# A first block of a transformer: another order for its opening stage, and two RMS norms' inverse roots moved from the operands to the products

## The chip, the cores and the metric

The kernel runs on one core of one Trainium2 chip. The metric is device time in microseconds (us) of one execution. Three runs of the kernel before gave 2043.5, 2043.73 and 2045.62 us, so the median is 2043.73 us. Engines: PE is the matrix engine (PEld its weight loads), DVE the vector engine, ACT the scalar engine, POOL the general engine, SP the engine that issues most transfers.

## The reference, cut to what matters

```
h = rmsnorm(x, norm_mix);  x = x + s5_mixer(h, ...)          # state space model, gelu, y @ w_glu, a * sigmoid(g)
x = x + sqrelu_mlp(rmsnorm(x, norm_ffn), mlp_w1, mlp_w2)     # relu(h @ w1)^2 @ w2
gate = sigmoid(rmsnorm(x, norm_ple) @ ple_gate_w);  x = x + (p @ ple_w) * gate
x = rmsnorm(x, norm_final)
... two more layers (w_ada_2 modulation, four mixer branches, swiglu), final norm
rmsnorm(x, g) = x * rsqrt(mean(x*x) + eps) * g               # mean over the 1024 features of a token
```

x is 256 tokens by 1024 features, everything in float32. The mixer is a linear recurrence with 64 groups of 16 features and 64 complex states, run here over 32 chunks of 8 tokens.

## The kernel before, in words

Each engine runs its own hand-written program, and semaphores tie them together. All big products ("phases" glu, mlp1, mlp2, ple and then those of the two layers) go through `gemm_pe` (L2487). A weight block of 1 MB lands in one of four ring slots of `raw`. ACT rounds each half of it into `wh` (`split_hi`, L799), POOL subtracts for the rest, `wl` (L2478), and PE takes three products per tile: xh\*wh, xl\*wh, xh\*wl (L2490 to L2492). SP loads the ring in the order of `RINGSEQ`: slot g is loaded again when block g-4 is used. Between the weights stand the 48 blocks of `w_ada`, each used once by `ada_block` (L649, 16 matmul records). Blocks 0 to 11 come first in the ring, ahead of the glu weights. After glu and after mlp2 come three blocks (`ada_tail`, run at the end of `gemm_pe`), then two weight blocks of the next phase, then a fourth ada block, whose slot is that of the second of the three.

**Opening.** While x loads, PE runs five unread products (`warm(5, 3)`, L2557, two records each). Then it transposes x (L2564) and x by group (L2570, which ends in `s_U`), the C matrices (L2578, `s_ct5`), the chunk factors (L2583) and the vectors (L2588). DVE builds b (to L2836), the factors F in four groups (`f_group`, 8.8 us each with a scratch in PSUM), U (L2895, after group 0), two products for the skip gain (L2902), the scan over chunks S (L2941 to L2959) and the last quarter of E (`e_group(3)`, L2855 to L2857). POOL builds the other three quarters of E. PE turns F pair by pair (`w1_transposes`, L2600), ACT copies each pair (L2294), PE multiplies it with U (`v_products`, L2611), and ACT copies V (L2285). Ada blocks 0, 1 and 2 come after pairs 8, 16 and 24. Then `k_products` (L2635, two halves), the skip product (L2660), `k_back` (L2648), which gives the lags K that ACT copies (L2306), and ada blocks 3, 4, 5. SP waits for that copy before it goes on with ring block 7, and issues seven transfers that shift the lags into the Toeplitz operand `toep` (`toep_dma`, L621). SP filled `toep` with zeros earlier, after `s_ct5` (L733), and only then began the ring. `y_products(d)` for d = 0 to 7 (L2682 with toep, L2687 with S and E) waits for S and toep; ada blocks 6 to 11 stand between them. For each d DVE turns Y (L2966), and ACT and DVE take turns for the gelu: square (L2310), argument (L2973), tanh (L2314), gate (L2978), xh (L2319), xl (L2982). Glu's first products need xh, xl of d = 0 to 7 one after the other.

**Norms 0 and 1** stand between glu and mlp1, and between mlp2 and ple. `norm_pe` (L929) takes sums of squares (L946, L951), five unread products (L926), spreads the inverse roots over the partitions (`norm_spread_pe`, L966) and runs the fourth ada block (`late`). DVE has the root chain (`rms_head_dve`, L1012) and then per feature tile x \* gain \* root (L1112), ACT rounds that to xh (L1094), DVE subtracts for xl (L1123). Mlp1 starts when the first tile is there.

Of the kernel before, what the change touches and what calls it, by code (L numbers as in the profile page):

```python
# [106 lines left out]
def build(nc, A, out, spill):  # L107
    ctx = ExitStack()
    with ctx:
# [119 lines left out]
        wsq = sqr[:, 2, SEQ:2 * SEQ]  # L229
        arena2 = part_m.mark[0]  # L230
# [131 lines left out]
        s_T = sem("toeplitz_placed")  # L362
# [18 lines left out]
        s_r = sem("relu_ready")  # L381
# [175 lines left out]
        HOME = {0: 40, 1: 40, 7: 40, "layer": 40}  # L557
# [29 lines left out]
        TOEP_AT = 7  # L587
# [28 lines left out]
        def toep_dma(sp):  # L616

            sp.wait_ge(s_Kc, 2)
# [40 lines left out]
        def ada_select(pe, i):  # L659

            pe.wait_ge(s_ac, i + 1)
            for b in range(2):
                ins = nc.tensor.matmul(ada_out[i][:, 32 * b:32 * b + 32], adat[:, b * P:b * P + P],
                                       const[:, C_SEL:C_END], start=True, stop=True)
            ins.then_inc(s_at, 1)

# [13 lines left out]
        def _(sp):  # L680
# [53 lines left out]
            for g in range(len(RINGSEQ)):  # L734
# [3 lines left out]
                if g == TOEP_AT:  # L738
                    toep_dma(sp)
# [362 lines left out]
        def norm_dve(dve, T1, n, gain, ring, dg, shift=None):  # L1102
# [6 lines left out]
            for k in range(KD + 1):  # L1109
# [7 lines left out]
                if k:  # L1117
# [11 lines left out]
                    ins.then_inc(s_xl, 1)  # L1129

# [1086 lines left out]
        def _(act):  # L2217
# [36 lines left out]

            def f_row_zero(r):
# [5 lines left out]
                for ri in range(2):  # L2261
                    nc.scalar.copy(Fg[r][:, :, ri, 0, :], Bb[:, ri, 8 * r:8 * r + 8, :]).then_inc(s_F0, 1)

            act.wait_ge(s_ct5, 1)
# [3 lines left out]
            act.wait_ge(s_fp5, 1)  # L2268
            nc.scalar.copy(fac[:, :], gb[:, 3, 0:NCH]).then_inc(s_fac, 1)

            f_row_zero(0)
            f_row_zero(1)
            act.wait_ge(s_vt, 1)
            nc.scalar.copy(vecs[:, :], gb[:, 1, 0:480]).then_inc(s_vc, 1)
            act.wait_ge(s_vc, 1)
            act.wait_ge(s_vz, 2)
            A1.add(nc.scalar.activation(sc[:, :, 30:31], vecs[:, V_C:V_C + 8].rearrange("p (k o) -> p k o", o=1),
                                        ACT.Tanh, scale=0.5))
            A1.add(nc.scalar.activation(sc[:, :, 31:32], vecs[:, V_CC:V_CC + 8].rearrange("p (k o) -> p k o", o=1),
                                        ACT.Tanh, scale=0.5))  # L2280
            A1.wait()
            act.sem_inc(s_th, 1)
            def v_copy(r):
                act.wait_ge(s_w1u, 8 * (r + 1))
                nc.scalar.copy(V[:, :, :, 8 * r:8 * r + 8].rearrange("p c r q -> p q r c"),  # L2285
                               mb[:, r, :].rearrange("p (q r c) -> p q r c", r=2, c=NCH)).then_inc(s_Vc, 1)

            f_row_zero(2)
            f_row_zero(3)
            for q in range(PAIRS):  # L2290
                act.wait_ge(s_w1t, q + 1)
                if q >= 4:
                    act.wait_ge(s_w1u, q - 3)
                nc.scalar.copy(w1[:, q % 4, :, :], gb[:, 1 + q % 2, 0:256].rearrange("p (r m) -> p r m", r=2))\  # L2294
# [4 lines left out]
            for i, banks in enumerate((gb[:, 1:3, :], mb[:, 2:4, :])):  # L2299
                act.wait_ge(s_KT, i + 1)  # L2300
                nc.scalar.copy(KT[:, 2 * i:2 * i + 2, :, :], banks.rearrange("p b (r n) -> p r b n", r=2))\
                    .then_inc(s_KTc, 1)
            act.wait_ge(s_K, 1)
            lags = toep[:, CH - 1, :, :].rearrange("p (q b) h -> p b q h", b=2)
            for b in range(2):
                nc.scalar.copy(lags[:, b, :, :], mb[:, b, :].rearrange("p (q h) -> p q h", h=GH)).then_inc(s_Kc, 1)  # L2306

            def gelu_square(d):
                act.wait_ge(s_yv, d + 1)
                nc.scalar.activation(gl[:, d % 2, 1, :], gl[:, d % 2, 0, :], ACT.Square).then_inc(s_y2, 1)  # L2310
# [6 lines left out]
            def gelu_hi(d):  # L2317
                act.wait_ge(s_yg, d + 1)
                nc.scalar.mul(xh[:, d, home("glu", SEQ)], gl[:, d % 2, 3, :], 0.5).then_inc(s_xh, 1)  # L2319

            for d in range(KD):
# [4 lines left out]
                if d == 5:  # L2326
                    act.wait_ge(s_E, 4)
                    act.wait_ge(s_S, 1)
                if d > 4:
                    for h in ((0, 1), (0,), (1,))[d - 5]:  # L2330
                        split_hi(act, (p_glu, 0, (0, 1, 1)[d - 5]), h)

            gelu_hi(KD - 1)
            ada_copy(act, 0)
            gemm_act(act, p_glu, pair_tanh(act, p_glu, SEQ), tail=lambda: squares_act(act, 0, sqr), split_first=False)
            act.dma_start(pnat[:, :, :], A["p"][0, 0].rearrange("(a p) d -> p a d", p=P)).then_inc(s_p, 16)
            operand_act(act, 0, sqr)
# [10 lines left out]
            gemm_act(act, p_m2, lambda it, j: None, tail=lambda: squares_act(act, 1, sqr), split_first=False)  # L2348
# [4 lines left out]
            operand_act(act, 1, sqr)  # L2353
# [14 lines left out]
            gemm_act(act, p_pl, pair_tanh(act, p_pl, SEQ), context_copy,  # L2368
# [118 lines left out]
        def gemm_pe(pe, p, T, X, need=None, after=None, lead=()):  # L2487
# [23 lines left out]
            def turn(it):  # L2511
                for j in range(p.body):
# [8 lines left out]
                    for b in range(2):  # L2521
# [10 lines left out]
                        ins.then_inc(mm_done, 1)  # L2532
                    i = it * p.body + j
# [11 lines left out]
        def _(pe):  # L2545
# [14 lines left out]
            warm(5, 3)  # L2560
# [12 lines left out]
            pe.wait_ge(s_x1, 1)  # L2573
            pe.wait_ge(s_cnat, 16 * 8)
# [5 lines left out]
            pe.wait_ge(s_small, 32)  # L2580
            pe.wait_ge(s_chk, 1)
            for a in range(2):
                ins = nc.tensor.matmul(gb[:, 3, GH * a:GH * a + GH], const[:, REP:CHK], chk[:, a, :], start=True, stop=True)  # L2583
            ins.then_inc(s_fp5, 1)
# [174 lines left out]
        def _(dve):  # L2759
# [226 lines left out]
            for d in range(KD + 1):  # L2986
                if d < KD:
                    turn_y(d)
# [110 lines left out]
```

## Time and profile before

| what | value |
|---|---|
| median of 3 runs | 2043.73 us |
| the profiled execution's own time | 2041.48 us |
| its span | 2039.7 us |
| PE busy | 1927.6 us, 95% |
| DVE, ACT, POOL busy | 932.9, 750.5, 1113.1 us |
| granted PE clock, mean | 0.965 of full |
| the opening, to the first glu product | 129.6 us |
| glu's last product, mlp1's first | 186.0 us, 198.3 us |
| mlp2's last product, ple's first | 410.7 us, 423.5 us |

"Busy" is the sum over an engine's instructions. The granted clock is a share of full speed: 0.50 is 1.2 GHz, 1.00 is 2.4 GHz. PE is busy for all but 112 us of the span.

### The profile page before, as it was taken

How to read it: one execution, taken by the hardware profiler on the slowest of the kernel's cores; microseconds unless marked ns; L12 is line 12 of the kernel's file. 1: busy time of each engine (PE TensorE's matmuls, PEld its weight loads, DVE VectorE, ACT ScalarE, POOL GpSimd, SP SyncE). 2: the span in 40 equal slices, each digit the busy share in tenths (PEclk: the TensorE clock that was granted, in tenths of full speed). 3: DMA queues.
4: the chain of work that ended last, by engine and by line, in shares of the span. 5: the costliest groups of instructions: out<-in, count | busy, mean ns of one | idle time of the engine just before them, and what ended most of it. 6: DMA issues, size and time to landing. Idle time of an engine off the chain costs nothing.

```text
span 2039.7 us, 33055 instructions
## 1 busy us (share of the span) xinstructions
PE 1927.6 (95%) x13867; PEld 1697.2 (83%) x13867; DVE 932.9 (46%) x1677; ACT 750.5 (37%) x1209; POOL 1113.1 (55%) x611
## 2 busy tenths in 40 slices
PE   6879999989999999999999999999999998989997
PEld 4558899987988689878777888888898997989997
DVE  7955441164555693662344111113557756363112
ACT  4333443233233722452323222222335526434443
POOL 6536777764344544344352444444368754777885
PEclk7779999999999999899998999999999999999999
DMA  7376788876213032212421323322255331555653
GB/s 162 117 259 218 262 285 270 278 247 218 80 46 107 14 114 73 63 32 93 144 93 62 104 78 109 103 80 85 90 159 156 110 109 32 179 167 165 183 179 101
DMA packets 299706, 276.72 MB, mean 136 GB/s; under 512 B 19771, under 2 KB 296773, under 8 KB 299301
## 3 DMA queue, kind: packets, MB, share of 16 engines
q1 hardware_dynamic: 297044, 271.43, 42.3%
q10 hardware_dynamic: 2192, 2.77, 0.4%
q8 instruction: 110, 1.80, 0.4%
q0 software_dynamic: 320, 0.40, 0.1%
q14 instruction: 40, 0.32, 0.0%
HBM read 266.70 MB, written 4.19 MB: 133 GB/s over the span
## 4 chain that ended last, share of the span: by engine, by line
PE 83%; DVE 8%; ACT 3%; POOL 2%; issue 2%; DMA 2%; SPq 1%; DVEq 0%; ACTq 0%; POOLq 0%
PE gb L2490 18%; PE gb L2492 17%; PE gb L2491 17%; PE gb L1443 4%; PE gb L1445 4%; PE gb L1444 4%; PE gb L1667 3%; PE gb L1669 3%; PE gb L1668 3%; PE mb L649 2%; POOL wl L2478 2%; PE mb L1175 1%; ACT wh L799 1%; PE mb L1242 1%; DMA raw<-in_w_ada 1%
## 5 line engine op out<-in xcount | busy, mean ns | idle before, releaser
L2478 POOL TENSOR_TENSOR wl<-raw,wh 128x1024 fp32r<-128x1024 f32 (+3 forms) x452 | 980.9, 2188 | 836.5 <-ACT wh L799 836.3
L799 ACT CAST wh<-raw 128x1024 fp32r<-128x1024 f32 (+3 forms) x452 | 418.9, 938 | 738.4 <-PE gb L2492 357.1
L2490 PE MATMUL gb<-xh,wh 128*128 128x256 f32 (+1 forms) x1856 | 604.3, 326 | 16.5 <-DVE xl L1125 6.7
L2491 PE MATMUL gb<-xl,wh 128*128 128x256 f32 (+1 forms) x1856 | 599.9, 323 | 0.0
L2492 PE MATMUL gb<-xh,wl 128*128 128x256 f32 (+1 forms) x1856 | 599.6, 323 | 0.0
L2490 PEld LDWEIGHTS gb<-xh,wh 128*128 128x128 f32 x1856 | 352.3, 190 | 55.5 <-issue 14.9
L2492 PEld LDWEIGHTS gb<-xh,wl 128*128 128x128 f32 x1856 | 352.2, 190 | 27.7
L2491 PEld LDWEIGHTS gb<-xl,wh 128*128 128x128 f32 x1856 | 352.4, 190 | 27.2
L1443 PE MATMUL gb<-wh,xh 128*128 128x256 f32 x608 | 174.7, 287 | 1.4 <-POOL wl L2478 1.3
L1444 PE MATMUL gb<-wh,xl 128*128 128x256 f32 x608 | 172.9, 284 | 0.0
L1445 PE MATMUL gb<-wl,xh 128*128 128x256 f32 x608 | 172.8, 284 | 0.0
L1443 PEld LDWEIGHTS gb<-wh,xh 128*128 128x128 f32 x608 | 117.5, 193 | 3.3 <-issue 3.2
L1667 PE MATMUL gb<-fhh,wh 128*128 128x512 f32 (+1 forms) x352 | 118.2, 336 | 0.0
L1444 PEld LDWEIGHTS gb<-wh,xl 128*128 128x128 f32 x608 | 117.5, 193 | 0.3 <-issue 0.2
L1669 PE MATMUL gb<-fhh,wl 128*128 128x512 f32 (+1 forms) x352 | 117.8, 335 | 0.0
L1668 PE MATMUL gb<-fhl,wh 128*128 128x512 f32 (+1 forms) x352 | 117.7, 334 | 0.0
L1445 PEld LDWEIGHTS gb<-wl,xh 128*128 128x128 f32 x608 | 117.4, 193 | 0.0
L2166 DVE SCALAR_TENSOR_TENSOR x<-gb,mod,x 128x256 f32<-128x256 f32 x72 | 31.9, 480 | 167.5 <-PE gb L1669 136.5
L2490 PE MATMUL gb<-brh,wh 128*128 128x512 f32 (+1 forms) x256 | 87.3, 341 | 7.9 <-POOL wl L2478 4.3
L2491 PE MATMUL gb<-brl,wh 128*128 128x512 f32 (+1 forms) x256 | 87.0, 340 | 0.0
L2492 PE MATMUL gb<-brh,wl 128*128 128x512 f32 (+1 forms) x256 | 86.9, 340 | 0.0
L2188 DVE SCALAR_TENSOR_TENSOR pr<-th,gb 128x1024 f32<-128x1024 f32 (+1 forms) x22 | 21.0, 955 | 136.0 <-ACT th L1801 136.0
(460 smaller groups left out, 2924.0 us busy)
## 6 DMA issues: line engine op xcount, KB each, us to landing
raw<-in_w_in SPq DMA_DIRECT2D x62, 1024.0 KB, 5.3
raw<-in_w_ada SPq DMA_DIRECT2D x48, 1024.0 KB, 6.7
raw<-in_w_ffn SPq DMA_DIRECT2D x44, 1024.0 KB, 5.1
raw<-in_mlp_w SPq DMA_DIRECT2D x32, 1024.0 KB, 5.2
raw<-in_w_ffn SPq DMA_DIRECT2D x16, 768.0 KB, 4.6
raw<-in_w_ffn SPq DMA_DIRECT2D x16, 640.0 KB, 4.2
raw<-in_ssm_w_glu SPq DMA_DIRECT2D x8, 1024.0 KB, 6.3
raw<-in_w_out SPq DMA_DIRECT2D x8, 1024.0 KB, 5.1
```

Of the source, the lines that this page charges most:

```text
L649: ins = nc.tensor.matmul(o[c:c + 32, :], sc[:, k, 30 - 2 * b:62 - 2 * b], W[:, k, :], start=(b == 0 and k < 4), stop=(n == n1 - 1 and k >= 4))
L799: nc.scalar.copy(split_half(wh, p, j, h), raw_half(p, it, j, h)).then_inc(hi_ready, 1)
L1443: nc.tensor.matmul(g[:, t, :], xh[:, k, ts], H[:, k], start=(k == 0), stop=False)
L1444: nc.tensor.matmul(g[:, t, :], xl[:, k, ts], H[:, k], start=False, stop=False)
L1445: ins = nc.tensor.matmul(g[:, t, :], xh[:, k, ts], L[:, k], start=False, stop=(k == KD - 1))
L1667: nc.tensor.matmul(o, H[:, kk, :], XH, start=(k == 0), stop=False)
L1668: nc.tensor.matmul(o, H[:, kk, :], XL, start=False, stop=False)
L1669: ins = nc.tensor.matmul(o, L[:, kk, :], XH, start=False, stop=(k == kt - 1))
L2478: nc.gpsimd.tensor_tensor(split_half(wl, p, j, h), raw_half(p, it, j, h), split_half(wh, p, j, h).bitcast(F32), ALU.subtract)\
L2490: nc.tensor.matmul(o, H[:, k, :], XH, start=st, stop=False)
L2491: nc.tensor.matmul(o, H[:, k, :], XL, start=False, stop=False)
L2492: return nc.tensor.matmul(o, L[:, k, :], XH, start=False, stop=sp_)
```

## The change

In the opening:

- `warm(5, 3)` becomes `warm(32, 3)`, and `warm(2, 2)` ahead of the pairs is gone.
- DVE makes F group 0 right after b with a scratch in SBUF, one group of six operations, before it takes the norm's root; the small operations for `aS` move ahead of the wait for U. PE multiplies the chunk factors before it transposes C; ACT copies rows 0 of F and the factors before C, and takes the silu's tanh at pair 4.
- The pairs turn over three PSUM banks instead of two. Ada blocks 0, 1, 2 stand ahead of pairs 8, 16, 24. `k_products(0)` and ACT's copy of it stand ahead of pair 24, in the middle of the loop.
- The lags come in two halves with a bank each, and ACT, not SP, issues the transfers into toep: seven per half, 2 KB rows instead of 4 KB. SP's ring is not held up at block 7.
- Ada blocks 3 to 11 all stand ahead of `y_products(0)`. The wait for S comes after the first Toeplitz products. The last quarter of E is made by DVE in two halves, after `turn_y(0)` and after `turn_y(1)`.
- Y and the gated value lie in PSUM banks (`y_view`, `gated_view`) instead of SBUF. The first weight splits for glu come at d = 3 to 6 instead of 5 to 7.

At norms 0 and 1: xh and xl are made from x \* gain without the inverse root, tile by tile, behind the residual of the phase before. The sums of squares are multiplied inside the first weight block of mlp1 and of ple (at k = 6), the spread comes after half a block (mlp1) or after block 1 (ple), and DVE copies the spread root to SBUF (`rb`). At the eviction DVE multiplies by `rb`: for mlp1 max(product, 0) \* rb, then ACT squares; for ple product \* rb, then ACT takes the tanh. The fourth ada block comes right after the three others. The five unread products of each norm are gone. Mlp1's lead goes from three half blocks to two, and its operands get an offset of 256.

The diff, cut to its core:

```diff
-        HOME = {0: 40, 1: 40, 7: 40, "layer": 40}
+        HOME = {0: SEQ, 1: 40, 7: 40, "layer": 40}
...
+        def toep_dma(act, i):
+            act.wait_ge(s_Kc, 2 * (i + 1))
+            here = slice(32 * i, 32 * i + 32)
             for j in range(CH - 1):
                 low = GH * (CH - 1 - j)
-                sp.dma_start(toep[low:P, j, :, :], toep[0:P - low, CH - 1, :, :]).then_inc(s_T, 16)
+                act.dma_start(toep[low:P, j, here, :], toep[0:P - low, CH - 1, here, :]).then_inc(s_T[i], 16)
...
-                if g == TOEP_AT:
-                    toep_dma(sp)
...
+        def operand_early_dve(dve, n, gain, k):
+            nc.vector.tensor_scalar(scaled[:, k % 4, :], x[:, k, 0:SEQ], gain(k, 0), None, ALU.mult).then_inc(s_xn, 1)
+        def operand_early_lo_dve(dve, n, k):
+            dve.wait_ge(s_xh, op0[n] + k + 1)
+            nc.vector.tensor_tensor(xl[:, k, home(n, SEQ)], scaled[:, k % 4, :], xh[:, k, home(n, SEQ)].bitcast(F32),
+                                    ALU.subtract).then_inc(s_xl, 1)
+        def root_to_sbuf_dve(dve, T1, n, dg):
+            rms_head_dve(dve, T1, n, dg, D, EPS)
+            dve.wait_ge(s_rb, n + 1)
+            T1.add(nc.vector.tensor_copy(rb, mb[:, 0, 0:SEQ]))
...
             for q in range(PAIRS):
+                if q == 4:
+                    silu_tanh()
+                if q == 24:
+                    turn_lags(0)
                 act.wait_ge(s_w1t, q + 1)
...
+            turn_lags(1)
+            copy_lags(0)
+            copy_lags(1)
+            ada_copy(act, 0)
...
             def relu(it, j):
-                multiplied(act, p_m1, it, j)
-                nc.scalar.activation(two(th, j % 2, SEQ), gview(p_m1, j, SEQ), ACT.Relu)\
-                    .then_inc(drained[unit(p_m1, j)[0]], 1)
+                wait_drained(act, p_m1, it, j, 1)
+                nc.scalar.activation(two(pr, j % 2, SEQ), two(th, j % 2, SEQ), ACT.Square).then_inc(s_r, 1)
...
-            warm(5, 3)
+            warm(32, 3)
...
-            warm(2, 2)
-            pe.wait_ge(s_vc, 1)
...
+            BEFORE = {8: (0,), 16: (1,), 24: (2,)}
             pe.wait_ge(s_Uc, 1)
             for q in range(PAIRS + 1):
+                for n in BEFORE.get(q, ()):
+                    if n == 0:
+                        pe.wait_ge(s_sc, 1)
+                    ada_block(pe, n)
+                if q == 24:
+                    pe.wait_ge(s_w1, 24)
+                    pe.wait_ge(s_Vc, 2)
+                    k_products(0)
                 if q < PAIRS:
                     w1_transposes(q)
                 if q:
                     v_products(q - 1)
             pe.wait_ge(s_w1, PAIRS)
             k_products(1)
+            skip_products()
             k_back(0)
             k_back(1)
-            for n in range(3, 6):
+            for n in range(3, FIRST_ADA):
                 ada_block(pe, n)
...
             for d in range(KD):
                 y_products(d)
-                if 6 + d < FIRST_ADA:
-                    ada_block(pe, 6 + d)
...
             gemm_pe(pe, p_glu, SEQ, X2("glu", SEQ), operand(0), selection(0, 0))
-            norm_pe(pe, 0, sqr, diag, lambda: ada_block(pe, ada_tail["glu"][3]))
-            gemm_pe(pe, p_m1, SEQ, X2(0, SEQ), operand(1), lead=THREE)
+            ada_block(pe, ada_tail["glu"][3])
+            def first_mlp(it, j, k):
+                if it == 0 and j == 0:
+                    if k == 6:
+                        norm_sums_pe(pe, 0, sqr)
+                    pe.wait_ge(s_xl, 8 + k + 1)
+            def first_spread(it, j):
+                if it == 0 and j == 1:
+                    norm_spread_pe(pe, 0, diag)
+            gemm_pe(pe, p_m1, SEQ, X2(0, SEQ), first_mlp, lead=THREE[0:2], mid=first_spread)
...
-            norm_pe(pe, 1, sqr, diag, lambda: ada_block(pe, ada_tail["mlp2"][3]))
+            ada_block(pe, ada_tail["mlp2"][3])
...
             for d in range(KD + 1):
                 if d < KD:
                     turn_y(d)
+                if d < 2:
+                    e_half(3, d)
...
-                    wait_drained(dve, p_m1, it, j, 1)
-                    v.tensor_tensor(two(pr, s, SEQ), two(th, s, SEQ), two(th, s, SEQ), ALU.mult).then_inc(s_r, 1)
+                    multiplied(dve, p_m1, it, j)
+                    v.scalar_tensor_tensor(two(th, s, SEQ), gview(p_m1, j, SEQ), 0.0,
+                                           rb.unsqueeze(1).to_broadcast([P, 2, SEQ]), ALU.max, ALU.mult)\
+                        .then_inc(drained[unit(p_m1, j)[0]], 1)
```

## Rows read from the trace of the kernel before

**Rows 1.** Four stretches, all engines: length, busy us (count), PEclk, DMA share, GB/s.

```profile
98.70:108.50 9.80, 0.07 (x7) 0.05 (x5) 7.32 (x7) 0.00 (x0) 0.00 (x0) 0.61 0.97 226
...
108.50:127.00 18.50, 18.47 (x480) 12.08 (x480) 12.27 (x24) 9.84 (x19) 0.00 (x0) 0.84 1.09 382
...
185.00:200.00 15.00, 12.30 (x113) 8.83 (x111) 8.96 (x23) 5.52 (x8) 9.52 (x4) 0.89 0.81 281
...
212.00:300.00 88.00, 87.24 (x795) 79.64 (x794) 44.14 (x27) 40.85 (x53) 69.77 (x27) 1.00 0.86 281
```

**Rows 2.** Chain of waits, at the ends of glu and of mlp2: start, us, what.

```profile
188.04 8.31 DMA raw<-in_w_ada
...
196.39 1.93 PE mb L649 x16
...
413.53 8.00 DMA raw<-in_w_ada
```

**Rows 3.** Timeline of PE, opening: start, us, engine, line, operation, operands, count, idle before.

```profile
4.01 6.82 PE L2557 MATMUL gb<-ones 128*128 128x512 f32 x10
...
24.63 3.67 PE L2564 MATMUL gb<-const,xnat 128*128 128x128 f32 x16 [13.79 <-DMA xnat<-in_x]
...
28.23 4.59 PE L2570 MATMUL mb<-const,xg 32*128 32x32 f32 x64
```

**Rows 4.** Timeline of PE's weight loads, two of the unread products.

```profile
9.38 0.19 PEld L2557 LDWEIGHTS gb<-ones 128*128 128x128 f32 x1 [0.24 <-issue]
...
9.81 0.19 PEld L2557 LDWEIGHTS gb<-ones 128*128 128x128 f32 x1 [0.24 <-issue]
```

**Rows 5.** Timeline of SP's queue, opening.

```profile
34.83 7.34 SPq L733 DMA_DIRECT2D toep<-zeros  x7
...
42.22 30.59 SPq L606 DMA_DIRECT2D raw<-in_w_ada  x7
```

**Rows 6.** DMA issues to 130 us: count, KB each, median us to landing.

```profile
raw<-in_w_ada SPq DMA_DIRECT2D x12, 1024.0 KB, 8.2
```

**Rows 7.** Timeline of DVE, opening.

```profile
39.12 2.29 DVE L2895 TENSOR_TENSOR U<-mb,fac 128x2048 f32<-128x2048 f32 x1 [0.22 <-DVE F L2883]
...
50.36 0.34 DVE L2870 COPY gb<-pw 128x56 f32<-128x56 f32 x2
...
79.23 0.29 DVE L2941 COPY S<-V 128x256 f32<-128x256 f32 x1 [0.86 <-ACT V L2285]
...
99.07 1.23 DVE L2855 TENSOR_TENSOR E<-pw,Ct 128x1024 f32<-128x1024 f32 x1 [0.21 <-DVE S L2959]
...
110.77 0.65 DVE L2966 STREAM_TRANSPOSE gl<-mb 128x256 f32<-128x256 f32 x1 [4.43 <-PE mb L2687]
...
114.61 0.66 DVE L2966 STREAM_TRANSPOSE gl<-mb 128x256 f32<-128x256 f32 x1 [2.27 <-PE mb L2687]
...
116.50 0.42 DVE L2982 SCALAR_TENSOR_TENSOR xl<-gl,xh 128x256 fp32r<-128x256 f32 x1
...
125.77 1.11 DVE L2966 STREAM_TRANSPOSE gl<-mb 128x256 f32<-128x256 f32 x1
...
136.90 2.35 DVE L2982 SCALAR_TENSOR_TENSOR xl<-gl,xh 128x256 fp32r<-128x256 f32 x1 [0.83 <-ACT xh L2319]
```

**Rows 8.** Timeline of ACT, two copies of a transposed pair.

```profile
55.30 0.37 ACT L2294 COPY w<-gb 128x256 f32<-128x256 f32 x1 [0.82 <-PE gb L2600]
...
74.23 0.37 ACT L2294 COPY w<-gb 128x256 f32<-128x256 f32 x1 [0.35 <-PE gb L2600]
```

**Rows 9.** Timeline of PE: K products, K turned back, norm 0's sums and spread.

```profile
77.91 1.96 PE L2635 MATMUL gb<-F,Ct 64*32 64x128 f32 x120
...
87.62 7.09 PE L2648 MATMUL mb<-const,KT 128*128 128x64 f32 x32
...
188.77 1.05 PE L946 MATMUL mb<-ones,sqr 128*128 128x1 f32 x8
...
194.08 0.71 PE L966 MATMUL mb<-const,diag 128*128 128x128 f32 x4 [1.10 <-DVEq L1023]
```

More of the change, by code:

```diff
@@ L361, in build @@
         s_yv = sem("Y_transposed_to_features")
-        s_T = sem("toeplitz_placed")
+        s_T = [sem(f"toeplitz_half_placed{i}") for i in range(2)]
         s_T0 = sem("toeplitz_zeroed")
@@ L2253, in _, with copy_lags, turn_lags @@
             nc.scalar.copy(x[:, :, 0:SEQ], gb[:, :, :].rearrange("p b (k t) -> p (b k) t", k=2)).then_inc(s_x1, 1)
+            def copy_lags(i):
+                act.wait_ge(s_K, i + 1)
+                lags = toep[:, CH - 1, :, :].rearrange("p (q b) h -> p b q h", b=2)
+                for b in range(2):
+                    nc.scalar.copy(lags[:, b, 16 * i:16 * i + 16, :],
+                                   lag_view(i, b).rearrange("p (q h) -> p q h", h=GH))\
+                        .then_inc(s_Kc, 1)
+                toep_dma(act, i)
+            def turn_lags(i):
+                act.wait_ge(s_KT, i + 1)
+                banks = ((mb[:, 1, :], mb[:, 3, :]), (gb[:, 1, :], gb[:, 2, :]))[i]
+                for b in range(2):
+                    ins = nc.scalar.copy(KT[:, 2 * i:2 * i + 2, b, :], banks[b].rearrange("p (r n) -> p r n", r=2))
+                ins.then_inc(s_KTc, 1)
             def f_row_zero(r):
@@ L2298, in _ @@
             v_copy(3)
[L2299 to L2306, printed above, removed]
+            turn_lags(1)
+            copy_lags(0)
+            copy_lags(1)
+            ada_copy(act, 0)
             def gelu_square(d):
                 act.wait_ge(s_yv, d + 1)
-                nc.scalar.activation(gl[:, d % 2, 1, :], gl[:, d % 2, 0, :], ACT.Square).then_inc(s_y2, 1)
+                nc.scalar.activation(gl[:, d % 2, 1, :], y_view(d), ACT.Square).then_inc(s_y2, 1)
             def gelu_tanh(d):
@@ L2532, in turn @@
                         ins.then_inc(mm_done, 1)
+                        if mid is not None and b == 0:
+                            mid(it, j)
                     i = it * p.body + j
@@ L2573, in _ @@
             pe.wait_ge(s_x1, 1)
+            pe.wait_ge(s_small, 32)
+            pe.wait_ge(s_chk, 1)
+            for a in range(2):
+                ins = nc.tensor.matmul(gb[:, 3, GH * a:GH * a + GH], const[:, REP:CHK], chk[:, a, :], start=True, stop=True)
+            ins.then_inc(s_fp5, 1)
             pe.wait_ge(s_cnat, 16 * 8)
@@ L2639, in k_products, with skip_products @@
                 ins.then_inc(s_KT, 1)
+            def skip_products():
+                pe.wait_ge(s_KTc, 1)
+                pe.wait_ge(s_sk, 1)
+                for i in range(2):
+                    for b in range(2):
+                        nc.tensor.matmul(lag_view(i, b), ident[0:GH, :],
+                                         Db[:, 2 * i:2 * i + 2].rearrange("p k (q b) h -> p b k q h", b=2)[:, b],
+                                         start=(b == 0), stop=False)
             def k_back(i):
@@ L2838, in _, with outer @@
             dve.sem_inc(s_Bb, 1)
+            def outer(dst, r, low, ri, op):
+                q, J = slice(8 * r, 8 * r + 8), dst.shape[2]
+                shape = [P, 8, J, GH]
+                pj = [pw[:, 1:J + 1, k, q].rearrange("p j q -> p q j").unsqueeze(3).to_broadcast(shape) for k in range(2)]
+                lw = [low[:, k, q, 0:GH].unsqueeze(2).to_broadcast(shape) for k in range(2)]
+                tmp = tE[:, 0:8 * J * GH].rearrange("p (q j h) -> p q j h", q=8, h=GH)
+                D1.add(v.tensor_tensor(dst, pj[0], lw[ri], ALU.mult))
+                step(v.tensor_tensor(tmp, pj[1], lw[1 - ri], ALU.mult))
+                step(v.tensor_tensor(dst, dst, tmp, op))
+            for ri, op in ((0, ALU.subtract), (1, ALU.add)):
+                outer(Fg[0][:, :, ri, 1:CH, :], 0, Bb, ri, op)
+            dve.sem_inc(s_F, 1)
             dve.wait_ge(s_ss, 1)
@@ L2906, in _ @@
             dve.wait_ge(s_T0, 16 * (CH - 1))
[L2907 to L2912 removed]
+            step(v.memset(S[:, 0, :, :], 0.0))
             G4 = NCH // 8
```

231 lines of the change are left out of this document (129 added, 102 removed).

## The prediction

> **What bounds it now.** I read four stretches by engine first [rows 1]. In the long middle of mlp1 PE is busy for 87.24 of 88 us at full clock, so the steady phases have nothing to give (0.76 us), and a change outside PE can only move the opening and the borders between phases. In the opening, from 98.7 to 108.5 us, PE works 0.07 us while the DMA engines are 0.97 busy: Y waits for the shifted lags. From there to 127 us the DMA engines stay above full share at 382 GB/s.
>
> The chain of waits comes next [rows 2]. After glu's last product (186 us) it runs through two ada blocks, then 8.31 us in the load of the fourth ada block, then that block. It does not run through the norm. The same stands after mlp2, with 8.00 us. The reader should see that the norm's root, sums and spread all lie beside a transfer that PE waits for anyway. That transfer starts when the second tail block is used, and the change moves neither.
>
> **Opening, step by step.** Times are of the profiled execution.
>
> Unread products. Five took ten records and 6.82 us [rows 3]; at full clock a record follows the last after 0.43 us [rows 4]. Thirty-two are 64 records: 4.01 + 6.82 + 54 x 0.43 = 34.0 us. x is there at 24.6 us [rows 3], so PE comes 9.4 us late. The two sets of transpositions took 3.67 and 4.59 us, mostly at the half clock [rows 3]. At full clock they are between 4.1 and 8.3 us; I take 6.1, as their spacing is partly the weight load's. `s_U` comes at 40.1 us.
>
> DVE. F group 0 now falls into the time before, and so do the root and `aS`; all is done near 31 us and costs nothing as long as PE is late. With factors and copy (0.6 us) U runs from 40.7 to 43.0 us. Before it ended at 39.12 + 2.29 = 41.4 us [rows 7], so it is 1.6 us later, and the 9 us gained on DVE are spent by PE. A group of F is 50.36 - 41.4 = 8.9 us [rows 7]; groups 1 to 3 end at 52.0, 60.9 and 69.8 us.
>
> First ada block. SP puts the zeros (7.34 us of issue) behind `s_ct5`, and the ring behind the zeros [rows 5]. `s_ct5` moves from 34.8 to 41.4 us, so block 0 is asked for at 48.8 us instead of 42.2. A load of this kind lands after 8.2 us in the median [rows 6], and 1 MB at 382 GB/s [rows 1] needs at least 2.7 us. I take 6.7, nearer the median, which holds loads that stand behind others: 55.5 us. Block 0 now stands ahead of pair 8, so PE waits there from 50 to 55.5 us with F group 1 ready since 52.0.
>
> Pairs. At half clock ACT's copy follows a pair every 0.37 + 0.82 = 1.19 us, at full clock every 0.72 [rows 8]. After the wait: block 0 1.9 us as at half clock [rows 2], eight pairs 7.0 (some slow), block 1 half of that at full clock, eight pairs 5.8, block 2 the same half, that is 72.2 us. Then the first half of the K products, 1.96 us [rows 9], and ACT's copy of it, 1.1 (as a V copy), stand ahead of pair 24. Eight pairs, the last product and the V copy end at 82.6 us. The scan starts there instead of at 79.23 and takes 99.07 - 79.23 = 19.8 us [rows 7]: S at 102.4 us.
>
> K. After the loop (81.5 us): 2.0 for the second half, 1.1 for the skip product, and for turning K back between 3.5 and 7.09 us [rows 9], the latter at half clock. I take 3.6, as PE no longer waits in between: 88.2 us.
>
> Ada 3 to 11 ahead of Y. Four blocks are in the ring, and five must be loaded: 5.24 MB at 382 GB/s, 13.7 us. The shifts into toep held the engines for 9.8 x 0.97 = 9.5 us [rows 1] and now run beside. Together 23.2 us from 88.2: the last block lands at 111.4 and is used by 113.3 us. Y, before at 108.5, starts then, and S, ready at 102.4, hides. Here stalls go: what Y waits for next is the ring.
>
> Whose transfers come first does not change this total. The Trainium skill ("DMA: Bandwidth & Descriptors", Queues, rings and completion order) says that each engine takes turns between the queues of SP and ACT, packet by packet; by that the second half of the lags lands before ada block 11, and Y's start would stay at 113.3. No run here shows both queues loaded yet.
>
> From Y's start to the last xl: first turn after 110.77 - 108.48 = 2.3 us; then a turn 0.65, half of E 3 x 1.23 = 3.7, argument 0.4, again a turn and half of E, and three operations: 12.7 us. Six more d at (125.77 - 114.61) / 5 = 2.23 us are 13.4. The last gate, rounding and rest are 1.7. Sum 27.8 us; before it was 136.90 + 2.35 - 108.5 = 30.8 us, in spite of no E inside [rows 7]. Last xl: 141.1 us against 139.3. **Opening: +1.8 us.**
>
> Why the tail is shorter: `xl<-gl,xh` took 0.42 us while POOL was idle and 2.35 us while it split weights [rows 7]. With Y in PSUM I take the short one everywhere. The Trainium skill ("SBUF — State Buffer", SBUF: two separate sides) has the reason: DVE and POOL share a port pair that is locked for a DVE operation with two SBUF inputs. The trace agrees, with 0.42 against 2.35 us; without that rule the sum would keep some 3 us more.
>
> **Norms.** The wait for the fourth ada block stays; mlp1 still starts 12.3 us after glu's end. Removed from the path: nothing, as sums, unread products, root and spread lay under the load [rows 2]. Added: the sums, two lots of about 1.0 us [rows 9], now stand inside mlp1's first block, and the spread (0.71, of which 0.6 counts). Overlap with big products could hide half of it, and slow weight loads at half clock could double it; I take 2.5 us. With sums and unread products gone from there PE idles from 188.8 to 196.4 us, where before they filled part of it. In rows 1 this stretch has a mean clock of 0.89; after the idle 9.8 us ahead of Y the mean of 18.5 us was 0.84. More half-clock time costs 0 to 1.3 us, I take 0.6. DVE's eviction with `rb` and ACT's square lie beside PE, which needs 5.8 us per weight block against some 3.3 us of ACT. If `rb` came late, mlp1's third block would wait for its bank; root (3.3 us) and copy fit in the half block in between. Against this the later stall of 0.7 us may go [rows 1]. **Norm 0: +2.4, norm 1 in the same way (8.00 us, [rows 2]) +3.1 us.** The tile work that moves behind the residuals in glu and mlp2 costs nothing: PE is the bound there; without that cover it would be some 8 us each.
>
> **Sum.** 1.8 + 2.4 + 3.1 = +7.3 us on 2041.48, the profiled execution's own time, is 2048.8. The median of the runs stands 2.25 us above that execution, so 2051.0 us.
>
> **Rivals.**
>
> A, the opening gains. If block 0 lands by 52 us, PE keeps to F: the loop ends at 69.8 + 6.2 = 76 us, K at 82.7, and five loads that the lags don't slow let Y start near 100. The last xl is then at 125 to 127 us, -13 with +5 for the norms: -8, 2036. For it speaks that the median of 8.2 us holds loads that stood in a full queue [rows 6], while block 0 stands first; against it 23 us of transfers that must pass before Y. It decides whether Y waits for S or for the ring. 25%.
>
> B, PE stays at half clock. The waits before block 0, in the pairs and in Y leave PE partly idle. With 24 pairs at 1.19 instead of 0.72 the scan starts 9 us later still, and so does all behind it: +16 us, 2060. For it: the clock was 0.61 in the idle stretch and PE came out of it slow [rows 1]. 15%.
>
> C, the norms bring what their removal from the path suggests, so the change doesn't do so little as I say: the fourth block lands soon after the third. Each border loses up to 7.5 us; 2031 us. Against it, 8.31 and 8.00 us. 5%.
>
> D, all small: inline sums are mostly hidden, the opening comes out even. 2043.7 to 2046. 10%.
>
> **How the numbers follow.** My forecast has 45%, with a range of its own of 2045 to 2057 from the bounds of the transpositions, of turning K back and of the sums. About 0.2% (4.1 us) is what a measurement can tell from no change. Faster: A and C, 0.30. Within: D and the low quarter of the forecast, 0.22. Slower: the rest and B, 0.48. The range from 2036 to 2060 leaves out C, the outer halves of A and B.
>
> **What would show it.** In the changed profile: unread products to 34 us, U's end near 43, a PE wait before block 0 near 50 to 55, scan start near 82.6, Y's start near 113 with a DMA as what it waited for, last xl near 141; after glu and mlp2 a DMA wait of 7 us ahead of the fourth ada block, and 16 small products inside the first weight block. The forecast is wrong if Y starts right behind S, or if mlp1 starts less than 12 us after glu ends.

## The result, and the profile after

| | before | after |
|---|---|---|
| median | 2043.62 us (2043.43 to 2045.62) | 2068.51 us (2064.52 to 2074.47, 4 runs) |
| ratio | | 1.0121, 95% interval 1.0097 to 1.0145 |
| the profiled execution's own time, span | 2041.48, 2039.7 us | 2074.47, 2072.7 us |

The change is slower by 1.2%. The forecast was 2051.0 us, and its range ended at 2060. The profiled execution of after is its slowest run (the two profiles lie 33 us apart, the medians 25), so its stretches are read against each other and the size of the effect from the medians. These are the borders of the two profiles, read as the rows below are:

| us from the start | before | forecast | after |
|---|---|---|---|
| block 0 of the modulation | 51.5 | 55.5 | 58.0 |
| scan starts | 79.2 | 82.6 | 93.9 |
| K turned back | 94.6 | 88.2 | 102.2 |
| Y starts | 108.5 | 113.3 | 127.9 |
| last `xl` is done | 139.3 | 141.1 | 155.2 |
| glu's last product | 186.0 | | 200.9 |
| glu's last product to mlp1's first | 12.2 | over 12 | 11.2 |
| ple's first product to layer 0's first | 54.2 | about 57 | 66.7 |

From layer 0 to the end, where nothing was changed, after takes 5.7 us longer in this execution. The twelve kernels below have the same code there and take from 0.1 us less to 6.9 us more than before, so this differs by execution and is no part of the effect.

**The opening.** PE's timeline to 36 us, and SP's from 40 us (start, duration, engine and line, operation, count):

```profile
4.02 30.30 PE L2634 MATMUL gb<-ones 128*128 128x512 f32 x64
34.16 1.91 PE L2641 MATMUL gb<-const,xnat 128*128 128x128 f32 x16
```

```profile
43.09 7.37 SPq L754 DMA_DIRECT2D toep<-zeros  x7
50.51 9.87 SPq L608 DMA_DIRECT2D raw<-in_w_ada  x5
```

The unread products end at 34.3 us as forecast, and the zeros and the ring start 8.3 us later than in [rows 5]. Then comes what wasn't forecast. PE's timeline around the pairs, and PE's clock by stretches (length, then busy time of PE, weight load, DVE, ACT and POOL, granted clock, DMA share, GB/s):

```profile
57.97 1.93 PE L652 MATMUL gb<-raw,sc 128*32 128x256 f32 x16 [3.58 <-DMA raw<-in_w_ada]
...
80.79 1.94 PE L652 MATMUL gb<-raw,sc 128*32 128x256 f32 x16
82.66 2.82 PE L2702 MATMUL mb<-F,Ct 64*32 64x128 f32 x128
```

```profile
56.00:64.00 8.00, 6.04 (x48) 3.36 (x48) 7.47 (x20) 2.02 (x4) 7.66 (x5) 0.50 1.08 383
64.00:72.00 8.00, 8.00 (x71) 4.73 (x70) 7.54 (x15) 2.29 (x8) 7.70 (x4) 0.50 0.36 127
72.00:82.70 10.70, 10.70 (x101) 6.60 (x104) 3.94 (x3) 4.23 (x11) 10.51 (x5) 0.50 0.30 99
82.70:96.00 13.30, 12.47 (x355) 9.97 (x352) 1.98 (x6) 6.81 (x14) 3.97 (x2) 0.94 0.26 83
110.00:128.00 18.00, 8.28 (x84) 3.06 (x88) 3.44 (x5) 0.00 (x0) 0.00 (x0) 0.64 1.08 345
```

The first 24 pairs run at half clock to the end, although PE is busy all the time from 58 us. Turning K back, at a mean clock of 0.64, ends at 102.2 us.

Part of this belongs to the one execution. opening_only, a kernel below, has the same opening, and there the clock rose behind block 1, near 71.5 us. Blocks 0 to 2 on its PE, and blocks 0 and 2 in before:

```profile
57.16 1.93 PE L649 MATMUL gb<-raw,sc 128*32 128x256 f32 x16 [2.66 <-DMA raw<-in_w_ada]
...
68.57 1.94 PE L649 MATMUL gb<-raw,sc 128*32 128x256 f32 x16
...
76.98 1.07 PE L649 MATMUL gb<-raw,sc 128*32 128x256 f32 x16
```

```profile
51.52 1.94 PE L649 MATMUL gb<-raw,sc 128*32 128x256 f32 x16
...
71.31 1.07 PE L649 MATMUL gb<-raw,sc 128*32 128x256 f32 x16
```

From the start of block 0 to the end of block 2 it took 20.9 us, as long as before took (51.5 to 72.4), against 24.8 us here. Of the eight profiles with the rebuilt opening four have 20.9 to 21.0 us and four 24.8; the first sixteen pairs are at half clock in all eight. In opening_only K is turned back at 97.3 us, Y starts at 124.3 and the last `xl` is done at 151.4: still 12.1 us later than before, where after is 15.9 later.

Only behind K come the other blocks of the modulation, and the chain of waits from there is one of loads:

```profile
102.22 1.91 PE gb L652 x16
104.15 7.47 DMA raw<-in_w_ada
111.67 1.98 PE gb L652 x16
113.66 12.52 DMA raw<-in_w_ada
126.23 1.93 PE gb L652 x16
```

S is ready near 114 us and waits 14 us for PE. In the last row of the windows PE works 8.28 of 18 us while the DMA engines are full.

**The norms.** After glu nothing is gained, as forecast: PE waits 6.52 us for the fourth block, whose load takes 7.28 us in the chain of waits, where [rows 2] had 8.31. The surprise is the per-layer-embedding phase (ple). PE's timeline there, without the large products:

```profile
444.59 0.95 PE L965 MATMUL mb<-ones,sqr 128*128 128x1 f32 x8
445.40 1.03 PE L970 MATMUL mb<-ones,sqr 128*128 128x1 f32 x8
449.80 0.71 PE L985 MATMUL mb<-const,diag 128*128 128x128 f32 x4 [0.41 <-DVEq L1042]
453.84 1.06 PE L666 MATMUL mb<-const,adat 128*128 128x32 f32 x4 [3.33 <-ACT adat L660]
```

and ACT's, where one `th` holds up what is queued behind it:

```profile
447.70 1.05 ACT L818 CAST wh<-raw 128x1024 fp32r<-128x1024 f32 x1 [11.27 <-PE gb L2567]
451.95 0.63 ACT L2442 ACTIVATE th<-th 128x512 f32<-128x512 f32 x1 [3.21 <-DVE th L3106]
452.49 1.03 ACT L818 CAST wh<-raw 128x1024 fp32r<-128x1024 f32 x1
453.43 0.36 ACT L660 COPY adat<-mb 128x256 f32<-128x256 f32 x1
```

ACT's tanh waits for DVE's scaled gate, which waits for the root. Behind it stand the next weight copy and the copy of the modulation's sums, and PE waits 3.33 us for the latter.

### The profile page after: what moved, and what is told of

The parts are those of the page before. It is cut to its first block, busy times and chain, and to the rows that moved or that the text cites. A ratio compares the mean times of both kernels' runs of the same rounds, so it can differ in the third digit from the quotient of the medians.

```text
span 2072.7 us, 33130 instructions
## 1 busy us (share of the span) xinstructions
PE 1959.5 (95%) x13901; PEld 1713.5 (83%) x13901; DVE 918.9 (44%) x1669; ACT 750.7 (36%) x1213; POOL 1112.8 (54%) x611
## 4 chain that ended last, share of the span: by engine, by line
PE 87%; DVE 6%; ACT 2%; DMA 2%; issue 1%; POOL 1%; SPq 0%; DVEq 0%; ACTq 0%
PE gb L2565 18%; PE gb L2566 18%; PE gb L2567 18%; PE gb L1485 4%; PE gb L1486 4%; PE gb L1487 4%; PE gb L1710 3%; PE gb L1711 3%; PE gb L1709 3%; DMA raw<-in_w_ada 2%; PE mb L652 2%; PE gb L2634 1%; PE mb L1217 1%; PE mb L1284 1%; ACT wh L818 1%
```

## The experiments

Twelve kernels in three sets of four, each set beside runs of before on its chip (medians 2048.16, 2045.47 and 2044.45 us). Executions of one kernel lie up to 0.8% apart (before in the second set: 2039.41 to 2055.78 us), so I go by the ratios and their 95% intervals.

### Which half costs: opening_only and norms_only

Each is the kernel before with one half of the diff: the rebuilt opening, or the two norms.

> The kernel before with the opening of the changed kernel and its own norms. Theory (the opening costs some 16 us, by the late PE, the late first ada block, the half clock in the pairs and five ring loads ahead of Y; the norms cost the rest): last xl near 155 us, glu's last product near 201, total before + 13 to + 17 us. Rival (what stands behind Y is an accident of one slow execution): before + 5 or less. Norms: mlp1 starts 12.3 us after glu ends, as before.

> The kernel before with the two late roots and its own opening. Theory (the fourth ada block's load stays the wait; sums and spread stand in line; at ple the root comes late and ACT with it): norm 0 + 0 to + 3 us, norm 1 and ple + 9 to + 13 us, total before + 9 to + 14 us. Rival (my forecast of + 2.4 and + 3.1): before + 5.5 us. Rival (the norms gain what leaves the path): before - 8 or less.

Measured: opening_only 2064.23 us, ratio 1.0092 [1.0066, 1.0117]; norms_only 2055.9 us, 1.0044 [1.0026, 1.0061]. Together 1.36%, against 1.21% [0.97, 1.45] for both. The halves add up and neither needs the other. opening_only is where it was expected, 16.1 us above its before; norms_only, 7.7 us above, is just under the 9 expected, and its interval (5.3 to 12.5 us) still holds the 5.5 of my forecast. The trace is what tells them apart: in norms_only the stretch from ple's first product to layer 0 took 67.6 us, in opening_only 56.9.

### The unread products: warm16

```diff
-            warm(32, 3)
+            warm(16, 3)
```

> The changed kernel with 16 unread products instead of 32. They end near 20 us, before x lands. Theory (the late PE moves everything behind it one for one, through the zeros and the ring): s_U, block 0, the scan and Y's start all some 8.5 us earlier, last xl near 147, total 8 to 9 us under the changed kernel. Rival (Y waits for the ring, whose loads run at one rate whatever came before): Y's start less than 3 us earlier, total 0 to 3 us under it.

Measured: 2065.03 us, 1.0089 [1.0057, 1.0121]. U's products end at 33.98 instead of 40.23 us and block 0 is used at 50.73 (before: 51.5). Yet the scan starts at 86.74 us. PE's timeline says why: a wait ahead of block 0, then half clock until 78 us, and the first half of K's products ahead of the last pairs.

```profile
50.73 1.94 PE L652 MATMUL gb<-raw,sc 128*32 128x256 f32 x16 [2.60 <-DMA raw<-in_w_ada]
...
73.55 1.94 PE L652 MATMUL gb<-raw,sc 128*32 128x256 f32 x16
75.42 2.88 PE L2702 MATMUL mb<-F,Ct 64*32 64x128 f32 x128
```

So neither number of unread products gives the first sixteen pairs the full clock. The 32 cost 6 us at the start. The last `xl` comes at 149.5 us, 5.7 us earlier than in after, but only 1.9 earlier than in opening_only, which has all 32 and had the better clock. Neither expectation was met (Y starts 6.1 us earlier, the ratio is 0.3% lower), and the intervals of warm16 and after overlap: this pair alone shows no gain. spread_warm16 below does.

### The place of the blocks: spread and spread_psum

In both, three blocks of the modulation stand ahead of Y and six between its features, as before. spread puts y and the gated y back into SBUF; spread_psum leaves them in PSUM, in banks 1 and 2, so that the sums of the blocks in bank 3 are not in their way. In both, ACT copies these sums behind the gelu, and DVE no longer waits for that copy.

```diff
-            for n in range(3, FIRST_ADA):
+            for n in range(3, 6):
...
                 y_products(d)
+                if 6 + d < FIRST_ADA:
+                    ada_block(pe, 6 + d)
...
-            return gb[:, 1 + 2 * (d % 2), 0:SEQ]
+            return gb[:, 1 + d % 2, 0:SEQ]
```

> The changed kernel with three ada blocks ahead of Y and six between its parts, as before; the gelu's tiles go back to SBUF and the copy of the ada sums behind the gelu, since the accumulator shares their PSUM bank. Theory (five ring loads ahead of Y cost the time): Y starts at S, 113.6 to 115 us, instead of 127.9, and some of that is given back to POOL's port; last xl 145 to 149 us, total 6 to 10 us under the changed kernel. Rival (the ring is full either way and the glu weights come late instead): last xl 153 or later, total within 2 us of it.

> The changed kernel with the modulation blocks 6 to 11 between the features of Y again, as before has them, but with y and the gated y still in PSUM, in banks 1 and 2 instead of 1 and 3, so that the accumulator in bank 3 doesn't stand against them. Theory P (place of the blocks): six of the nine blocks ahead of Y are what delays Y, by waits for their loads (4.57, 4.64, 0.62, 1.12 and 1.67 us at PE) and 1.9 us each; spread got 11 us back at the last xl though VectorE's reads of y went back to 2.4 to 2.7 us from 0.42. With y in PSUM the tail from the first E products to the last xl falls from spread's 35 us to 28 to 31, so the last xl stands at 137 to 141 and the time is 2 to 6 us under spread, ratio 1.003 to 1.007. Rival (the loads decide): blocks 6 to 11 arrive at the DMA's rate, block 11 not before some 135, and the last xl cannot come before 142: ratio as spread's, 1.0076.

Measured: spread 2062.23 us, 1.0076 [1.0047, 1.0106], last `xl` at 143.8 us; spread_psum 2053.98 us, 1.0044 [1.0029, 1.0060], last `xl` at 135.4. Both are where their theories had them, or a little better. From after's 1.0121 to spread_psum's 1.0044: the place of the blocks is 0.8%, the largest single term, and the loads didn't forbid it. The difference of spread and spread_psum is DVE's argument of the gelu. In spread, late in Y:

```profile
135.57 2.35 DVE L3072 SCALAR_TENSOR_TENSOR gl<-gl 128x256 f32<-128x256 f32 x1 [0.55 <-ACT gl L2371]
...
139.66 2.35 DVE L3072 SCALAR_TENSOR_TENSOR gl<-gl 128x256 f32<-128x256 f32 x1 [0.57 <-ACT gl L2371]
```

In spread_psum the same operation, with y from PSUM:

```profile
131.06 0.42 DVE L3072 SCALAR_TENSOR_TENSOR gl<-gl,gb 128x256 f32<-128x256 f32 x1 [0.69 <-ACT gl L2371]
...
133.19 0.42 DVE L3072 SCALAR_TENSOR_TENSOR gl<-gl,gb 128x256 f32<-128x256 f32 x1 [0.69 <-ACT gl L2371]
```

The nine blocks ahead of Y were put there to free bank 3 for y. Bank 2 was free, and the short operations could be had without them.

### The two together: spread_warm16 and k_behind

spread_warm16 is spread_psum with 16 unread products. k_behind also puts the first half of K's products behind the pairs:

```diff
                 if q == 24:
                     pe.wait_ge(s_w1, 24)
-                    pe.wait_ge(s_Vc, 2)
-                    k_products(0)
...
+            pe.wait_ge(s_Vc, 2)
+            k_products(0)
             k_products(1)
```

> spread_psum with 16 unread products at the start instead of 32. warm16 alone started U 6.3 us earlier (33.98 against 40.23) and ended the opening 4.5 us earlier at the first product of the gated unit's end. Additive: 3 to 6 us under spread_psum; the price of the opening's change is then all but returned, and with the changed norms the ratio is 1.002 to 1.005. If it gives under 1.5 us, the start of the opening was hidden behind something that spread_psum leaves as the bound.

> spread_warm16 with the first half of the products of K behind the pairs, as before has them, instead of ahead of the last eight pairs. In warm16 PE's 24 pairs end at 75.4, then the half takes 2.88 us, then the last pairs 7.2 us, and the scan starts at 86.74 against 79.23 before, of which the half is 2.9. If the scan is on the path to Y: the scan starts 2.9 us earlier and the last xl 1 to 3 us earlier; if the chain K, copies, Toeplitz transfers or the loads of the modulation is what Y waits for, the last xl stays or comes later by up to 3 us. Ratio to spread_warm16 0.9985 to 1.001.

Measured: spread_warm16 2047.76 us, 1.0004 [0.9988, 1.0021]; its last `xl` is at 130.5 us, 9 us earlier than before, its glu ends at 174.8 instead of 186.0, and the changed norms then lose all of it again. It is 0.4% under spread_psum, a little more than expected, and the two intervals don't overlap: sixteen unread products are better than 32. k_behind 2045.03 us, 1.0007 [0.9992, 1.0021]: its scan starts at 77.3 instead of 84.2 us. Of these 6.8 us some 2.9 are the order; the rest is the clock of the pairs, 21.0 us from block 0 to the end of block 2 against 24.8. DVE's U ended at the same time in both (35.0 and 35.1 us). The last `xl` comes 2.2 us earlier (128.3 against 130.5), and in the ratio, 1.0007 against 1.0004, no gain shows. The order of K and the scan is worth nothing that can be measured once the blocks are spread.

### The norms' price: tanh_behind and sums_early

Both are norms_only with one thing changed. tanh_behind moves ACT's wait for the scaled gate behind the weight copies:

```diff
             def scaled_tanh(it, j):
-                if j % 2 == 0:
-                    wait_drained(act, p_pl, it, j, 1)
+                if j % 2:
+                    wait_drained(act, p_pl, it, j - 1, 1)
...
+                if i == 1:
+                    wait_drained(pe, p_pl, 0, 0, 1)
```

sums_early puts the sums, the unread products and the spread back between the third and the fourth block (`norm_pe` as before), and keeps the rest of the changed norms.

> The kernel before with the norms of the changed one (norms_only), and in the per-layer-embedding phase ScalarE takes the tanh of a gate one weight block later, behind the copies of the next block's halves; PE waits for the gate's scaled eviction before it transposes the context. Theory W (weights): norms_only loses its time there because ScalarE stands 3.2 us at the scaled gate (th at 436.72 behind VectorE's eviction at 436.00), with the second half of the next weight block (437.25) and the copy of the sums of the modulation (438.19) queued behind it; the ring's slots come free late and the DMA share of 433 to 442 is 0.00 against 0.43 before. Then the weight copy starts near 434, the stretch from the phase's first product to the layers' first falls from 67.6 us to 58 to 61 (before: 54.2), and the time is 6 to 9 us under norms_only's 2055.9, ratio to before 1.000 to 1.002. Theory I (inline work): it is the sums and the spread between the products, 1.0 + 1.0 + 0.7 us, and the clock that falls after the wait for them; then ScalarE's order changes 2 us at most and the ratio stays 1.003 to 1.0045.

> The kernel before with the norms of the changed one, but the sums, the root and the spread stand where before has them, with the five unread products between them, ahead of the fourth block of the modulation, in both norms; the root is still applied at eviction and the operands are still made in the phase ahead. Theory W: the root is ready when the first gate is, so ScalarE's wait for the scaled gate is one eviction, 0.7 us, and the time is within 2 us of before (ratio 0.999 to 1.001). Theory I: the same, since no work is left between the products. If it stays at 1.003 or above, neither holds and the scaled evictions themselves (0.69 us more per pair on VectorE, in front of ScalarE's tanh) are the price.

Measured: tanh_behind 2048.85 us, 1.0019 [1.0001, 1.0036]. ple to layer 0 fell from 67.6 to 59.9 us, as Theory W had it; the ratios alone (1.0044 and 1.0019) overlap in their intervals. Nine microseconds from some 10 us behind ple's first product, in norms_only and then in tanh_behind (columns as in the windows above):

```profile
433.00:442.00 9.00, 5.25 (x30) 4.86 (x29) 7.06 (x14) 2.96 (x6) 5.99 (x3) 0.76 0.00 0
```

```profile
431.00:440.00 9.00, 7.47 (x50) 7.15 (x50) 5.76 (x13) 2.64 (x6) 6.96 (x4) 0.81 0.33 115
```

The DMA share of 0.00 is the damage: with the weight copies held up the ring's slots stayed full and nothing was loaded for 9 us, ahead of a border that waits for loads. After has 0.01 in the same place, from 447 to 456 us.

sums_early missed: 2053.94 us, 1.0049 [1.0031, 1.0068], where both theories said about 1.000. Its ple phase was indeed short, 56.8 us, but from mlp2's last product to ple's first it took 18.5 us, where before took 12.7:

```profile
417.73 0.95 PE L949 MATMUL mb<-ones,sqr 128*128 128x1 f32 x8
422.09 1.87 PE L954 MATMUL mb<-ones,sqr 128*128 128x1 f32 x8 [3.41 <-ACT sqr L878]
423.81 4.58 PE L929 MATMUL gb<-ones 128*128 128x256 f32 x10
428.97 0.71 PE L969 MATMUL mb<-const,diag 128*128 128x128 f32 x4 [0.57 <-DVEq L1026]
```

The changed kernel had dropped `split_first=False`, so ACT makes the first weight copies of the next phase, which wait for their load until 418.9 us, ahead of the last squares (421.4 us; 411.7 before). The expectation blamed the scaled evictions for a ratio of 1.003 or above; the phase in which they stand took 2.6 us more than before, the border 5.8. So the old place of the sums needs the old order of ACT. That is read from this trace; no run had the two together.

### Two covers: late_block and norms_late

The fourth block is used behind the first weight block of the next phase; late_block does this to the kernel before, norms_late to tanh_behind, with the spread right behind it. The edit of norms_late at norm 0 (norm 1 alike):

```diff
-            ada_block(pe, ada_tail["glu"][3])
+            def first_spread(i):
+                if i == 0:
+                    ada_block(pe, ada_tail["glu"][3])
+                    norm_spread_pe(pe, 0, diag)
```

> The kernel before with its norms as they are, the fourth block of the modulation behind the first weight block of the next phase instead of ahead of it (both norms). Before, PE waits 8.3 and 8.0 us for this block by the chain of waits, but the operands of the norm are made in the same time. Theory: the load hides the norm and the norm hides the load, so taking the block away gives back only what the load is longer: 0 to 2 us at each norm, 0 to 4 in all (ratio 0.998 to 1.000). Rival: the block's slot comes free some 6 us later, the ring stands, and the phase waits for weights later: ratio 1.000 to 1.003.

> tanh_behind with the fourth block of the modulation and then the spread behind the first weight block of the next phase, in both norms: the first products then wait for neither the norm nor this load. Theory L (two covers): the norms of the changed kernel could not gain because the load of the fourth block ends at the same time as the old norm did; without both, the first product of mlp1 stands at 188 to 191 instead of 195.9 and that of the per-layer phase at 415 to 419 instead of 423; 3 to 7 us at each, of which the half clock takes some back: 4 to 10 us under tanh_behind, ratio 0.995 to 0.999. Rival R (the ring decides): weights and blocks come at the rate of the DMA, whatever the order in which they are read; the products start earlier and wait later, and the time is within 2 us of tanh_behind.

Measured, with tanh_behind as the fourth corner:

| | block ahead | block behind |
|---|---|---|
| old norms | 1 | 1.0023 [1.0009, 1.0038] |
| new norms | 1.0019 [1.0001, 1.0036] | 0.9977 [0.9964, 0.9990] |

Either alone makes it slower by 0.2%, both together faster by 0.2%. late_block came where its rival had it, norms_late in its expected range. The border after glu shows the two covers. late_block, PE:

```profile
181.47 2.80 PE L649 MATMUL mb<-raw,sc 128*32 128x256 f32 x48
...
189.51 0.71 PE L966 MATMUL mb<-const,diag 128*128 128x128 f32 x4 [1.10 <-DVEq L1023]
...
193.81 0.35 PE L2490 MATMUL gb<-xh,wh 128*128 128x256 f32 x1 [2.29 <-DVE xl L1123]
```

norms_late, PE:

```profile
183.15 2.80 PE L652 MATMUL mb<-raw,sc 128*32 128x256 f32 x48
...
186.51 0.36 PE L2531 MATMUL gb<-xh,wh 128*128 128x256 f32 x1 [0.56 <-issue]
```

Without the load the old norm takes the wait over, and the border is 12.3 us as before. Without both it is 3.4 us, 8.8 less. Of these, mlp1 and mlp2 gave back 2.8 us (219.0 us for them against 216.2) and ple 2.9. At the second border, from mlp2's last product to ple's first, next to nothing was gained, 12.3 us against 12.7, where I expected 3 to 7: PE stood 7.88 us there, to 414.03 us, with no releaser shown. ACT and POOL tell what it was:

```profile
407.97 1.99 ACT L802 CAST wh<-raw 128x1024 fp32r<-128x1024 f32 x2 [17.48 <-DMA raw<-in_ple_gate_w]
409.09 4.83 POOL L2519 TENSOR_TENSOR wl<-raw,wh 128x1024 fp32r<-128x1024 f32 x2 [15.34 <-ACT wh L802]
```

The first product waits in the program for both halves of ple's own first weight block (`w_ready`, L2540). Their load lands at 408.0 us, and POOL is done with the second half at 413.9. So here a third cover lay under the other two.

### A version that beats both: best_mix

spread_warm16 with the norms of norms_late.

> spread_warm16 with the norms of norms_late: the late fourth block, the spread behind it, and the tanh of the gate one block later. The norms gave back 0.67% against norms_only (1.0044 to 0.9977) on the opening of before. If openings and norms stay additive: 0.67% under spread_warm16, ratio 0.996 to 0.999 to before, 25 to 30 us under the changed kernel. If the ring has to catch up after either repair, the two overlap and the ratio is 1.000 to 1.003.

Measured: 2029.74 us (2026.14 to 2033.58), 0.9918 [0.9896, 0.9939]. The border after glu is 3.3 us, and layer 0 starts at 466.3 us, 11.4 before the kernel before. The parts add up: it is 0.86% under spread_warm16 where norms_late stood 0.67% under norms_only, and below the expected 0.996 to 0.999.

## Why the prediction was wrong

Direction and places were right, the size was not: +7.3 us forecast, +25 measured. By its own steps:

**Right.** Unread products to 34.0 us (34.3), `s_U` at 40.1 (40.2), U's end at 43.0 (41.53 + 2.29 = 43.8). From K turned back to the use of the last block 23.2 + 1.9 us was forecast; it was 128.2 - 102.2 = 26.0, though the lags went by ACT's queue beside the ring. The tail from Y to the last `xl` was to be 27.8 us and was 155.2 - 127.9 = 27.2: the operations with y in PSUM took 0.42 us beside a busy POOL. The Trainium skill's rule on the port pair that DVE and POOL share ("SBUF — State Buffer", SBUF: two separate sides) was the right reason to take the short value, and spread against spread_psum shows it by 2.35 against 0.42 us. The fourth block did hold the borders.

**Wrong, the opening's +1.8 us, by the step "Pairs".** The last `xl` came 15.9 us later than before (12.1 in opening_only). I let the clock rise within the first eight pairs behind block 0 (7.0 us for them, then 5.8), with 72.2 us for the end of block 2; it was 82.7. Block 0 came 2.5 us later than forecast, 1.7 of it because C was turned by 43.0 us and not by 41.4, at half clock already. The half clock of the pairs cost the other 8.0. K's first half took 2.82 for 1.96 us, and K's turning back 5.75 for 3.6. These are 13.5 of the 14.0 us that bring K's end from 88.2 to 102.2 us, and the loads for the nine blocks hang on that, since a slot comes free only when its block is used. In opening_only 4.2 of the 8.0 us are left, K ends at 97.3 and Y starts at 124.3 us, 11 us over the forecast: so about half of the clock's cost belongs to after's one execution, and the step was wrong without it too. Before's own trace had 20.9 us from block 0 to the end of block 2, for which I put 16.7. This is rival B, to which I gave 15%; its pairs, 9 us, were nearly right for after's profile, and its total of +16 lacked the rest of the norms. I had read the clock of [rows 8] as a property of the kernel. It isn't: in norms_late, whose opening is the one before, the stretch from 56 to 64 us ran at full clock. PE then waited 1.95 us for DVE's F and fell back to half clock, and its scan started no earlier (80.6 us).

**Wrong, the step "Norms", norm 1.** The term of +3.1 us measured +12.5 from ple to layer 0 (+13.4 in norms_only). I costed the eviction with `rb` as "beside PE" and asked only whether the bank came free. What stood behind ACT's wait for that eviction, weight copies and the modulation's copy, wasn't followed, nor the ring behind these. tanh_behind returned 7.7 of 13.4 us by that order alone. The step of norm 0 (+2.4) was too high: after has 1.0 us less at the border and 1.3 more in the two phases.

**Right, but half read.** "It does not run through the norm" is what the chain said, and so the removal gained nothing. That two equal covers lie on top of each other, which the chain can't show, is what norms_late used; rival C asked for the load to be gone and gave it 5%, and I didn't see that the block could be moved.

What stays open: why the granted clock rises earlier in one execution of the pairs than in another, with the same code; and why late_block is slower than before, though its border is no longer. Mlp1's lead of two half blocks instead of three and the operands' offset were not run alone.

## What to carry to other kernels

Where the chain of waits runs through a load, look for the second thing that ends at the same time: take away both or neither, since each alone can measure slower, and then look for a third, such as the next phase's own first weights. When an engine that also feeds a ring gets a new wait, list what is queued behind it and follow the ring to the next border; a DMA share of zero in a phase that streams weights is the sign. And before a group of loads is moved ahead of a stage to free a bank, look for another bank.

## What the runs showed of the hardware

PE stayed at half clock while it was busy. In after it worked without a break from 58.0 to 82.7 us, and the granted clock was 0.50 in all of it. In opening_only the same code rose near 71.5 us, in before near 66.5 us, in sums_early, whose opening is that of before, near 76.7, and in norms_late near 53.4. The fall is as plain: in after PE was busy without a break from 4.0 to 43.0 us, the first thirty of these microseconds with unread products at full clock, and still the clock fell near 40 us, at the end of the 64 transpositions of 32x32 and ahead of the first wait. The Trainium skill ("TensorE: Matmul & The Clock Gate", Part 1: The HAM clock gate) says of the array that "the default state is throttled, and activity releases the throttle"; by that I would expect full clock within the pairs. These traces don't agree, and the measurement decides. The unread products ahead of this stage bought nothing for its pairs.

The second thing is the spread of the start. With the same code up to there, x's transposition began at 22.8 us in k_behind and at 25.8 in warm16, by the arrival of x. So marks of the opening are compared from there, and on the engine that the next step waits for: PE's products for U ended at 28.8 us in k_behind and at 30.9 in spread_warm16, by the clock, and DVE's U ended at 35.0 and 35.1.
